# Expert weights in 16 KB runs and a second landing place for expert rows, in a decoder layer with grouped experts

## The reference, cut to what matters

```python
u = rms_norm(x, norm2_g[l]) * (1.0 + sc2) + sh2
x = x + g2 * grouped_moe(u, w_router, moe_w1[l], moe_w3[l], moe_w2[l])

def grouped_moe(u, w_router, w1, w3, w2):      # 16 experts, 4 groups, D 1024, D_EXPERT 512
    aff = softmax(xt @ w_router)
    # best group by the sum of its top-2 affinities, then the top-2 experts inside it
    gate = ...                                  # 512 x 16, two entries a row, normalised
    for e in range(N_EXPERTS):
        h = jax.nn.silu(xt @ w1[e]) * (xt @ w3[e])
        y = y + gate[:, e:e + 1] * (h @ w2[e])
```

## Time and profile before

| | us |
|---|---|
| median of 3 runs | 746.54 (744.59 to 747.54) |
| the profiled execution | 745.55 |
| its span, first to last instruction | 743.7 |

### The profile page before, as it was taken

The page is one execution under the profiler, slowest core; times in us unless marked ns, Lnnn a source line. Parts: engine busy times, 40 slices in busy tenths (PEclk is TensorE's granted clock), DMA queues, the critical chain, the costliest instruction groups (busy, mean ns, idle before and its releaser), DMA issues.

```text
span 743.7 us, 15473 instructions
## 1 busy us (share of the span) xinstructions
PE 596.7 (80%) x6189; PEld 356.1 (48%) x6193; DVE 342.9 (46%) x882; ACT 204.4 (27%) x440; POOL 82.5 (11%) x119
## 2 busy tenths in 40 slices
PE   0798999977689999789992089999989878999940
PEld 0544474565356666555441055555555444555520
DVE  4713819233179899952326033333333322333325
ACT  3300100113246767842222012222222211222200
POOL 6001000007100000000000401011111100111122
PEclk9998999987879999999996589999999989999985
DMA  8980957051299500038009729999999999999428
GB/s 332 376 317 7 394 222 274 9 185 52 89 344 232 157 1 1 1 115 339 1 0 332 285 90 315 371 368 376 370 368 371 375 378 380 373 374 374 166 63 310
DMA packets 81436, 176.38 MB, mean 237 GB/s; under 512 B 9426, under 2 KB 26394, under 8 KB 79354
## 3 DMA queue, kind: packets, MB, share of 16 engines
q1 hardware_dynamic: 68592, 152.90, 58.2%
q0 software_dynamic: 8384, 13.97, 5.6%
q10 hardware_dynamic: 4428, 9.07, 3.7%
HBM read 155.16 MB, written 20.71 MB: 236 GB/s over the span
## 4 chain that ended last, share of the span: by engine, by line
DMA 27%; PE 18%; DVE 5%; issue 3%; POOL 2%; SPq 1%; ACTq 0%; ACT 0%; POOLq 0%; DVEq 0%
DMA featT<-expert_rows 16%; DMA pool_sb<-in_moe_w 9%; PE score L1512 7%; PE score L1611 5%; PE score L1620 3%; DVE featT L1213 2%; SPq L461 1%; DMA pool_sb<-expert_rows,idx 1%; POOL expert_rows L776 1%; POOL pool_sb L796 1%; PE bank L1601 1%; DMA expert_rows<-pool_sb,idx 1%; DMA expert_rows<-featT 1%; PE bank L1547 0%; PE bank L1556 0%
## 5 line engine op out<-in xcount | busy, mean ns | idle before, releaser
L1611 PE MATMUL score<-pool_sb,featT 128*32 128x256 f32 x2688 | 159.3, 390 | 21.2 <-DMA pool_sb<-in_moe_w 10.1
L1611 PEld LDWEIGHTS score<-pool_sb,featT 128*32 128x32 f32 x2688 | 87.0, 112 | 90.2 <-issue 20.5
L685 ACT ACT_TABLE_LOAD x42 | 53.9, 1283 | 230.9 <-DVE featT L1213 195.6
L1308 PE MATMUL bank<-pool_sb,featT 128*128 128x512 f32 (+2 forms) x256 | 88.6, 508 | 5.8 <-DVE featT L851 2.6
L1620 PE MATMUL score<-pool_sb,featT 128*32 128x256 f32 x1344 | 81.2, 382 | 3.6 <-DMA pool_sb<-in_moe_w 2.8
L1308 PEld LDWEIGHTS bank<-pool_sb,featT 128*128 128x128 f32 x256 | 49.8, 196 | 43.1 <-issue 35.4
L1233 DVE TENSOR_TENSOR featT<-featT,score 128x128 f32<-128x128 f32 x42 | 12.1, 288 | 118.1 <-ACT featT L685 118.1
L784 POOL DMA_DIRECT2D expert_rows<-featT x42 | 31.7, 755 | 266.6 <-DVE featT L1227 254.5
L1213 DVE COPY featT<-featT 32x1024 f32<-32x1024 f32 x44 | 30.3, 689 | 60.1 <-DMA featT<-expert_rows 59.8
L1512 PE MATMUL score<-pool_sb,featT 128*128 128x512 f32 x128 | 56.9, 597 | 0.0
L1620 PEld LDWEIGHTS score<-pool_sb,featT 128*32 128x32 f32 x1344 | 39.6, 109 | 27.5 <-DMA pool_sb<-in_moe_w 3.1
(11 more groups left out here) (254 smaller groups left out, 636.9 us busy)
## 6 DMA issues: line engine op xcount, KB each, us to landing
pool_sb<-in_moe_w SPq DMA_DIRECT2D x48, 2048.0 KB, 22.4
pool_sb<-in_ada_w SPq DMA_DIRECT2D x16, 1024.0 KB, 6.5
expert_rows<-zeros_f SPq DMA_DIRECT2D x17, 512.0 KB, 6.6
featT<-expert_rows ACTq DMA_DIRECT2D x45, 128.0 KB, 5.5
expert_rows<-featT POOLq DMA_DIRECT2D x42, 128.0 KB, 7.5
pool_sb<-in_ada_w SPq DMA_DIRECT2D x8, 640.0 KB, 11.5
pool_sb<-in_w_out SPq DMA_DIRECT2D x4, 1024.0 KB, 16.7
pool_sb<-in_ada_w SPq DMA_DIRECT2D x8, 384.0 KB, 9.6
```

Source lines behind the costliest of these rows:

```text
L685: nc.scalar.activation(silu, banks[0][:, 0:HB], ACT.Silu).then_inc(m_si, 1)
L1308: m = nc.tensor.matmul(pj_bank(g, i)[:, 0:n], featT[:, k, i * P:(i + 1) * P], w_stage[:, g % 3, k, 0:n], start=(k == 0), stop=(k == KD - 1))
L1611: mm = nc.tensor.matmul(banks[0][h * BT:(h + 1) * BT, 0:2 * HB], xgT[:, k, :], w[:, :, :, h, :], start=(k == 0), stop=(k == KD - 1))
```

## The change

- **Landing places.** `xg_in` becomes a list of two, partitions 32 to 63 and 64 to 95, each with a semaphore of its own. ScalarE loads blocks 0 and 1 at once and issues the load of block g+4 when the copy of g+2 is made (before: g+3). VectorE's `rows_in(g + 2)` moves from behind `rows_out` to right behind `hidden(g)`, ahead of its wait for the outer product.
- **Weights.** The DRAM side is read as `(p k) n -> p k n`: a partition gets 8 (w1, w3) or 4 (w2) neighbouring rows, one run of 16 KB.
- **Order of the columns.** Piece k of the contraction now stands for the model's columns 8q + k. So `x_hat` writes the normalised rows permuted, its input read 8 elements (32 bytes) apart; the transposes give the matching columns. The scale and shift of the second modulation are needed in that order: TensorE transposes them (beside the router's bias row), VectorE copies the 16 rows, SP writes them to a small DRAM tensor and reads them back as `mod_rows_col`.
- **Hidden units.** TensorE's inner product takes 128 neighbouring units for each of its 4 groups (before: 4 runs of 32), and VectorE's product writes them 32 elements apart, so that the transposed piece c holds units 4p + c.
- **Constants.** GpSimd's semaphores for its constants are merged into one (`t_const`).

The diff without the declarations:

```diff
-        xg_in = blkbuf[BT:2 * BT, 0:D]
+        xg_in = [blkbuf[(1 + n) * BT:(2 + n) * BT, 0:D] for n in range(2)]
...
             def load_matrix(e, m):
                 done = e_w2[e % 3] if m == 2 else e_w13[e % 3]
                 sp.dma_start(chunk_of(e % 3, m, DE // P if m == 2 else KD),
-                             MOE_W[m][0, e].rearrange("(k p) n -> p k n", p=P)).then_inc(done, 16)
+                             MOE_W[m][0, e].rearrange("(p k) n -> p k n", p=P)).then_inc(done, 16)
...
             load_matrix(2, 1)
+            sp.wait_ge(r_ltc, 1)
+            sp.dma_start(mod_dram, mod_rows[:]).then_inc(s_mr, 16)
+            sp.wait_ge(s_mr, 16)
+            sp.dma_start(mod_rows_col[:], mod_dram.rearrange("(s a) (b k) -> (a b) s k", s=2, k=KD)).then_inc(s_mr, 16)
             sp.wait_ge(o_pj, 2 * TT)
...
-                nc.scalar.activation(norm_x[:, i, :], x_sb[:, i, :], ACT.Copy, scale=rstd2[:, i:i + 1]).then_inc(r_xh, 1)
+                nc.scalar.activation(norm_x[:, i, :].rearrange("p (k q) -> p k q", k=KD), x_sb[:, i, :].rearrange("p (q k) -> p k q", k=KD),
+                                     ACT.Copy, scale=rstd2[:, i:i + 1]).then_inc(r_xh, 1)
...
-            def xg_load(g):
-                act.dma_start(xg_in, xs[bass.ds(g * BT, BT), :]).then_inc(s_xg, 16)
-
-            def block_of_rows(g):
+            def xg_load(g, n):
+                act.dma_start(xg_in[n], xs[bass.ds(g * BT, BT), :]).then_inc(s_xg[n], 16)
+
+            def block_of_rows(g, n):
                 act.wait_ge(m_h1, g + 1)
                 nc.scalar.activation(silu, banks[0][:, 0:HB], ACT.Silu).then_inc(m_si, 1)
                 act.wait_ge(m_cp, g + 3)
-                xg_load(g + 3)
+                xg_load(g + 4, n)
...
                     dve.wait_ge(r_lt, 1)
+                    nc.vector.tensor_copy(mod_rows[:], banks[6][0:2 * KD, P:2 * P])
                     nc.vector.tensor_copy(bias_row[:], banks[6][:, 0:NE]).then_inc(r_ltc, 1)
...
                 nc.vector.tensor_tensor(xgT, banks[4][:, 0:KD * BT].rearrange("p (k r) -> p k r", k=KD),
-                                        mod_col[:, 16:24].unsqueeze(2).broadcast_to([P, KD, BT]), ALU.mult).then_inc(m_sc, 1)
+                                        mod_rows_col[:, 0, :].unsqueeze(2).broadcast_to([P, KD, BT]), ALU.mult).then_inc(m_sc, 1)
...
-                nc.vector.tensor_tensor(hmid, silu, banks[0][:, HB:2 * HB], ALU.mult).then_inc(m_h, 1)
+                nc.vector.tensor_tensor(hmid.rearrange("p (c a) -> p a c", c=NT), silu.rearrange("p (a c) -> p a c", c=NT),
+                                        banks[0][:, HB:2 * HB].rearrange("p (a c) -> p a c", c=NT), ALU.mult).then_inc(m_h, 1)
...
                     hidden(m * 2 + 1 + n)
+                    rows_in(m * 2 + 3 + n, 1 - n, m + 2 + n)
                     dve.wait_ge(m_y, m * 2 + 1 + n)
                     hmid_T(m * 2 + 1 + n)
                     dve.wait_ge(s_ys[n], m * 16)
                     rows_out(y_sb[n])
-                    rows_in(m * 2 + 3 + n)
...
-                m = nc.tensor.matmul(banks[6][:, 0:NE], ones[:], wr_shifted[:, k, :], start=(k == 0), stop=(k == KD - 1))
-            m.then_inc(r_lt, 1)
+                nc.tensor.matmul(banks[6][:, 0:NE], ones[:], wr_shifted[:, k, :], start=(k == 0), stop=(k == KD - 1))
+            nc.tensor.transpose(banks[6][0:2 * KD, P:2 * P], mod_col[:, 16:32], ident[:]).then_inc(r_lt, 1)
...
-                    w = exp_w13[slot][:, :, k, :].rearrange("p m (c h a) -> p m c h a", h=NT, a=BT)
+                    w = exp_w13[slot][:, :, k, :].rearrange("p m (h a) -> p m h a", h=NT)
```

68 lines of the change are left out of this document (36 added, 32 removed).

## The result

The changed kernel takes 741.02 us (median of 6 runs, 740.21 to 742.04), the kernel before in the same series 746.90 (744.59 to 748.31). The ratio is 0.9926, 95% interval 0.9906 to 0.9946: 5.5 us faster, where 11.4 were forecast. The profiled execution took 740.75 us (before 745.55), its span is 739.1 (before 743.7).

The account below looks back on a forecast made before the run. It took the weight stream to bound the kernel until block 27, then the row loop. -9.1 - 0.5 - 2.4 + 0.27 + 0.35 = -11.4 us gave 734.1 from the profiled run, 735.1 from the median; own range 730 to 739, overall 723 to 748.

Parts of the forecast that it names:

- What bounds the kernel: Expert stage: the weight stream decides when block 27 starts, the row load and copy loop how fast the rest runs.
- Price of the pieces: Weight stream before block 27: 16 KB pieces save 0.35 us a load over 26 loads, 9.1 us; bounds 0.12 and 0.55.
- 7.5 ns a piece and 37.9 ns a KB: Cost line per DMA engine through the 2 KB and 8 KB rows, giving 614 ns for 16 KB, thus 427 GB/s.
- rival (c): Weight stream gains much more, only TensorE's pace is left: 725.8 us, needs 1.1 us a load; chance 0.10.
- Rival (b): Weight stream: a piece costs about half the line's price, 0.17 us saved a load: 740.1 us; chance 0.13.
- Rival (a): Weight stream gains nothing in the crowd, the mixing with rows may hold it: 744.7 us; chance 0.15.
- Wait for w2 at block 27: TensorE's outer product at block 27: its 0.87 us wait for w2 shrinks, 0.5 us saved.
- Row loop behind block 27: Blocks 28 to 40: two landing places take row loads off the path, step becomes 5.93 us, 2.4 us saved.
- Moved copy: VectorE's row copy of 0.69 us fits in its 1.01 us gap before the outer product's wait; cost 0.
- Extra transpose: Ahead of the expert stage: TensorE's added transpose of the modulation columns lies on the path, costing 0.27 us.
- ScalarE's strided rows: Ahead of the expert stage: normalised rows read 32 bytes apart put 0.35 us on the path, bounds 0 and 0.95.
- Rival (d): Expert stage: large weight pieces delay small row transfers, fourfold queueing, loads landing after 15.5 us: 804 us; chance 0.07.

Follow-up runs that it names:

- places_only: Kernel before with two landing places and the moved copy, weights still in 2 and 4 KB pieces, nothing permuted: 745.98 us, ratio 1.0001.
- after_spread: Changed kernel with each block's 32 rows loaded into 128 partitions in 1 KB pieces, turned in two 128 x 128 transposes: 725.75 us, ratio 0.9704.
- after_halves: Changed kernel with each weight matrix loaded by two DMAs in 8 KB pieces: 738.84 us, ratio 0.9902.
- after_exp_first: Changed kernel with the router's exponential put ahead of ScalarE's last normalised rows: 741.32 us, ratio 0.9925.
- after_quarters: Changed kernel with rows still landing in 32 partitions, but each row in four 1 KB pieces with 64-byte gaps: 740.27 us, ratio 0.9904.
- halves_exp: Changed kernel with 8 KB weight pieces (two DMAs a matrix) and the router's exponential ahead of the last normalised rows: 739.21 us, ratio 0.9905.
- pieces_only: Kernel before with 16 KB weight pieces and the permuted columns, but one landing place and the copy where it was: 767.97 us, ratio 1.0289.

## Why the prediction was wrong

- **What bounds the kernel: right.** The stream decides until block 27. places_only moved nothing, after_spread took 14.1 us out of block 27's start by the stream alone.
- **Price of the pieces: the step that failed.** The forecast put a price read from lone streams on the crowded one: "I take 0.35" on 26 loads, for 9.1 us, and 4.2 came, 0.16 a load (block 27 at 173.76 instead of 177.96 behind block 1). For a lone stream 0.35 was about right: 434 GB/s were measured where 427 were forecast, and beside cheap row loads the pieces are worth 0.38.
- **That 0.35 is right there is luck.** The line "7.5 ns a piece and 37.9 ns a KB" does not pass through its own two rows. 83.4 and 316.6 ns give 38.9 ns a KB and 5.7 ns a piece, thus 628 ns for 16 KB, 418 GB/s, 0.26 us a load, and 6.7 us instead of 9.1. (The upper bound of 0.55, worked out again, is 0.42.) But the row of 8 KB pieces was another load's and slow for its size; the weights in 8 KB pieces go at 423 and 426 GB/s by themselves (after_halves), 309 ns a piece, and the line through that gives 609 ns and 0.38 us. One error made up for the other. What the crowd did came on top of both.
- **What the crowd did.** The "share of the row traffic's cost" which rival (c) named as something that might vanish did the opposite: the row loads' price rose from 0.64 to 0.84 us a weight load, since a 16 KB weight piece takes 0.680 us beside them instead of 0.61.
- **Rival (b) gave 740.1 and the median is 741.02, but by another mechanism.** Its 0.17 us a load is what the crowded stream shows, and what the Trainium skill's fixed 3 cycles a packet (DMA: Bandwidth & Descriptors, "Why small descriptors are slow") would give by the estimate in the prediction. Yet 434 against 385 and 401 GB/s in lone streams, and 0.38 beside spread rows, contradict that price: the match in the total is an accident. Rival (a)'s sentence, that what holds the stream "may be the mixing, not the pieces", named the real cause, with half its weight.
- **Rival (c)** asks for 1.1 us a load. By its own figures 0.63 would do: block 27 at 599.3 instead of 615.73 is 16.4 us over 26 loads. after_spread saves 0.66 and takes 725.75 us, (c)'s 725.8; it needed an edit that the change does not have.
- **Wait for w2 at block 27: right.** 0.87 became 0.37 us, 0.5 forecast.
- **Row loop behind block 27: right as mechanism, lost in this kernel's profile.** No wait for row loads is left, the step behind block 28 is 623.38 - 617.46 = 5.92. In places_only and after_halves blocks 28 to 40 take 74.3 and 74.4 us (73.8 forecast, 76.2 before). In the changed kernel they take 76.06, since TensorE stands 2.12 us at block 40 with "issue" as releaser, and its inner product then takes 5.35 us instead of 3.66, so block 41 starts 7.64 us behind block 40 instead of 5.95. The granted clock in that product is 0.68 in the mean (before the stand, and behind the product, it is 1.00, the level of 2.4 GHz):

```profile
693.52:698.87 5.35, 5.34 (x65) 2.85 (x66) 0.00 (x0) 0.00 (x0) 0.00 (x0) 0.68 0.12 32
```

  Beside the 0.48 us of other entries the stand thus costs 1.6 + 1.7 = 3.3 us. What stands there is its sequencer, reading the block bounds into a register; the line of that read in the changed kernel, 600 to 716 us, ns min/median/max:

```profile
L381 PEldq TENSOR_LOAD <-block_start x5: 300/306/1912, 605.6 to 691.0; - x5
```

  The same read took 1777 ns in after_exp_first and at most 306 in after_quarters, which has the same weight pieces. The medians fit its being a property of the kernel: 741.0 and 741.3 us for the two that have it, 738.8 and 739.2 for after_halves and halves_exp, which don't. What makes it slow was not found.
- **Moved copy, TensorE's operand in runs of 128: right,** the inner product is still 3.64 us. The strided product takes 378 ns instead of the 288 before, hidden.
- **Extra transpose:** 0.27 forecast, some 0.02 seen from one piece of the projection to the next, far below what executions differ by.
- **ScalarE's strided rows: mis-sized.** 0.35 was taken; the time of a call doubled, the case of the upper bound and one of the prediction's own signs of being wrong (over 2 us each):

```profile
394.88 2.14 ACT L670 ACTIVATE pool_sb<-x_sb,pool_sb 128x1024 f32<-128x1024 f32 x1 [1.62 <-POOL pool_sb L779]
396.93 0.24 ACT L685 ACTIVATE pool_sb<-pool_sb 128x64 f32<-128x64 f32 x1
```

  From the start of the last rows to the exponential 2.05 us, before 1.35, so 0.70 of delay. VectorE's windows were the wrong neighbour; the rule of cachelines in the Trainium skill (SBUF — State Buffer, "Door 1: The DMA port swizzle"), quoted in the prediction, agrees with ScalarE's time: it doubles. No other step than 32 bytes was tried. after_exp_first took the 0.7 away and the total didn't show it.
- **Rival (d), small transfers behind large pieces:** the mechanism is there, and pieces_only shows its price with one place, +21.5 us. Its size (a fourfold growth of the queueing) was too large: 3.3 us grew to 4.6 for loads, and stores went from 7.6 to 11.6. What was held against it, "the queueing seems to go by bytes", does not hold: the same 128 KB land after 6.9 us as 32 pieces and after 10.2 to 11.0 as 128 pieces beside 16 KB weights, but after 5.5 as 128 pieces beside small ones. Beside large pieces the wait grows with the number of the load's own pieces, beside small ones hardly (5.3 us as 32 pieces in places_only). The forecast had asked only what this does to row loads; the stores, with their two buffers, are the ones that came near the path.

The sum by its own terms, in the profiles, whose spans differ by 4.6 us: block 27 -4.2 (forecast -9.1), w2 -0.4 (-0.5), blocks 28 to 40 -0.2 (-2.4), the product behind the stand +1.7 (no term), the rest behind it +0.6 (no term). Block 1 itself starts 2.1 us sooner, which is within its scatter and hides the 0.7 of ScalarE's rows.

## What to carry to other kernels

A gain per piece read from a stream by itself holds beside other transfers only if those don't slow the stream's own pieces: look at how long a large piece takes alone and in the crowd before multiplying. Small transfers that run beside a saturated stream are worth landing in all 128 partitions; here that brought 15 us, nearly three times the change itself. They then need more time to land (10.2 us here), so look whether the places cover it. And larger pieces delay small transfers, so a second landing place belongs with them: either alone brought nothing or cost 21 us.

## What the runs showed of the hardware that was not expected

- A 16 KB weight piece took 0.61 us by itself, 0.680 in the mean beside row loads into 32 partitions, 0.664 beside the same rows in 1 KB pieces, 0.626 when they landed in 128, though the row loads' own share of the engines' time stayed at 6.0 to 6.2%.
- Lone streams: 385 to 401 GB/s with 2 KB pieces, 434 with 16 KB; with 8 KB 412 to 414 for the load at 118 us, but 423 and 426 for the weights. Of the 8 to 13% between 2 and 16 KB, 2 to 3% are left at 8.
- 2520 of the changed kernel's weight pieces had no piece of a row load beside them and took 0.629 us, 792 had more than 1.2 us of them and took 0.821.
- Row loads from issue to landing: 5.6 us beside 2 and 4 KB pieces, 5.8 beside 8 KB, 6.9 beside 16 KB; stores 7.6, 8.8 and 11.6. In 128 pieces of 1 KB instead of 32 of 4 KB: 10.2 to 11.0 beside 16 KB, 5.5 beside small ones.
- ScalarE read 128 x 1024 float32 with a step of 32 bytes in 2.14 us, contiguous in 1.15.
- A register read on TensorE's sequencer, 0.3 us elsewhere, took 1.8 to 1.9 us in two of the kernels, at one place.
